# Nine modulation blocks among the pool chunks instead of five, and every third tile of the first norm modulated by VectorE

## The reference

```python
for l in range(DEPTH):                                  # DEPTH = 2
    ada = jax.nn.silu(cond) @ w_ada[l] + b_ada[l]       # 1024 x 6144 weights a layer
    sh1, sc1, g1, sh2, sc2, g2 = jnp.split(ada[:, None, :], 6, axis=-1)
    u = layer_norm(x) * (1 + sc1) + sh1
    if l % 2 == 0:
        m, k, v = even_mixer(u, ...)                    # attention beside a pool mixer
    else:
        m = odd_mixer(u, ...)                           # gated conv beside a Fourier mixer
    x = layer_norm(DEEPNORM_ALPHA * x + g1 * (m @ w_out[l]), ln_g[l, 0], ln_b[l, 0])
    u = layer_norm(x) * (1 + sc2) + sh2
    f = conv_ffn(u, w_up[l], ffn_conv_w[l], ffn_conv_b[l], w_down[l])
    x = layer_norm(DEEPNORM_ALPHA * x + g2 * f, ln_g[l, 1], ln_b[l, 1])
```

## Time and profile before

| what | value |
|---|---|
| median of three runs | 2673.08 us (2669.34 to 2676.3) |
| the profiled execution | 2669.81 us |
| its span | 2668.0 us |
| TensorE busy | 2564.1 us, 96% of the span |
| VectorE busy | 1608.6 us, 60% |
| ScalarE busy | 1067.2 us, 40% |
| GpSimd busy | 462.8 us, 17% |
| moved by DMA | 294.43 MB, mean 110 GB/s |

### The profile page before, as it was taken

One profiled execution on the slowest core, in us unless ns is written; L12 is line 12 of the kernel. 1 busy time (PEld: TensorE's weight loads), 2 busy tenths in 40 slices (PEclk: granted clock), 3 DMA queues, 4 the chain that ended last, 5 costly groups with the idle time before them and its releaser, 6 DMA issues. The chain is left out here.

```text
span 2668.0 us, 35753 instructions
## 1 busy us (share of the span) xinstructions
PE 2564.1 (96%) x13380; PEld 2284.1 (86%) x13380; DVE 1608.6 (60%) x2415; ACT 1067.2 (40%) x1691; POOL 462.8 (17%) x269
## 2 busy tenths in 40 slices
PE   5799799999999999999999999999999999999998
PEld 2488588778999999987777999988999999997886
DVE  2326677768866666644676533257866666654665
ACT  4412577846433233333645511126533332323442
POOL 1160377726000000000222000016100000000212
PEclk7889799999999999999999999999999999999999
DMA  9920100023222222255665312122322222245564
GB/s 326 340 74 15 55 1 1 1 96 111 72 62 67 70 74 74 58 200 186 240 246 191 106 40 75 58 80 87 90 74 74 74 74 71 61 168 171 198 213 142
DMA packets 209365, 294.43 MB, mean 110 GB/s; under 512 B 11529, under 2 KB 146677, under 8 KB 209263
## 3 DMA queue, kind: packets, MB, share of 16 engines
q1 hardware_dynamic: 205892, 284.10, 32.5%
q0 software_dynamic: 2736, 8.01, 0.8%
q10 hardware_dynamic: 635, 0.94, 0.1%
HBM read 247.73 MB, written 45.29 MB: 110 GB/s over the span
## 5 line engine op out<-in xcount | busy, mean ns | idle before, releaser
L2988 PE MATMUL ps<-d_ring,hs 128*128 128x512 f32 x2376 | 557.8, 395 | 1.9 <-PE ps L2988 1.3
L2988 PEld LDWEIGHTS ps<-d_ring,hs 128*128 128x128 f32 x2376 | 445.8, 188 | 113.9 <-issue 9.4
L1741 DVE TENSOR_TENSOR d_ring<-d_raw,d_ring 128x1024 fp32r<-128x1024 f32 x132 | 180.7, 1369 | 227.3 <-ACT hs L1054 226.9
L1036 POOL TENSOR_TENSOR ey<-ey,gb_end 128x1024 f32<-128x1024 f32 x17 | 44.1, 2592 | 1490.0 <-ACT ey L1559 1490.0
L2831 PE MATMUL ps<-act_b,w_A 128*128 128x384 f32 x1584 | 282.4, 336 | 2.9 <-ACT fp L1054 1.6
L2831 PE MATMUL ps<-act_a,w_A 128*128 128x384 f32 x1584 | 282.4, 336 | 2.9 <-ACT fp L1054 1.6
L2831 PEld LDWEIGHTS ps<-act_a,w_A 128*128 128x128 f32 x1584 | 275.2, 188 | 3.6 <-ACT fp L1054 1.9
L2831 PEld LDWEIGHTS ps<-act_b,w_A 128*128 128x128 f32 x1584 | 275.1, 188 | 3.6 <-ACT fp L1054 1.9
L1054 ACT ACTIVATE d_ring<-d_raw 128x1024 fp32r<-128x1024 f32 x132 | 139.8, 1059 | 286.0 <-PE ps L2988 249.8
L2619 PE MATMUL ps<-act_b,uw 128*128 128x384 f32 x1440 | 250.8, 336 | 1.5 <-DVE act_b L1741 1.2
L2619 PEld LDWEIGHTS ps<-act_b,uw 128*128 128x128 f32 x1440 | 249.4, 188 | 2.2 <-DVE act_b L1741 1.5
(11 more groups left out here) (284 smaller groups left out, 4252.1 us busy)
## 6 DMA issues: line engine op xcount, KB each, us to landing
d_raw<-in_w_down SPq DMA_DIRECT2D x132, 512.0 KB, 3.4
ada_w<-in_w_ada SPq DMA_DIRECT2D x52, 512.0 KB, 6.6
h_rows<-fh SPq DMA_DIRECT2D x44, 576.0 KB, 3.6
h_raw<-h_rows SPq DMA_DIRECT2D x132, 192.0 KB, 3.7
raw_u<-in_w_up SPq DMA_DIRECT2D x44, 512.0 KB, 5.4
raw_odd<-in_w_up SPq DMA_DIRECT2D x40, 512.0 KB, 4.9
end_w<-in_w_ada SPq DMA_DIRECT2D x24, 512.0 KB, 7.5
late_w<-in_w_ada SPq DMA_DIRECT2D x20, 512.0 KB, 6.9
```

Of the source, the lines that this page charges most:

```text
L1036: chain(gp.tensor_tensor(y, y, gb_end[l][:, 0, :], ALU.mult))
L1741: return v.tensor_tensor(dst, src, hi.bitcast(F32), ALU.subtract)
L2988: mm = pe.matmul(out, h[:, a, tile % 3 * P:(tile % 3 + 1) * P], d[:, w, 512 * half:512 * half + 512], start=f == 0 and (a, w) == (0, 0), s ...
```

## The change

- Five modulation blocks (4 to 8) stay in the first norm and nine (9 to 17) go among the pool chunks: `ADA_LATE` is 9. `FIRST_ADA` puts the five behind the turns of tiles 0, 2, 3, 5 and 6; `LATE_CHUNKS` then has one late block behind each chunk from (0, 1) to (3, 0). Banks, evacuation steps and SP's order follow: SP's loop over the norm's rows is written out, with no block behind every third tile, and its late loads stand among the weight loads.
- Tiles 2, 5 and 8 are modulated by VectorE out of the same PSUM banks into a second row `in_u2`; ScalarE still rounds them.
- All four column products of the second norm and of layer 1 come behind the last pool chunk, from four buffers `bias_row`; the rotary tables wait for them.
- In the FFN's `behind`, `third(0, 1)` and `first_product(0, 1)` stand ahead of the roundings of S3 and S1.

```diff
-    return {s: [s + 2] for s in range(2, 11)} if kind == "in" else {}
+    return {2: [4], 4: [5], 5: [6]} if kind == "in" else {}
-ADA_LATE = 13
+ADA_LATE = 9
+def ada_bank_of(m):
+    if m < ADA_TOP:
+        return 3 + m % 3
+    return 5 if m == ADA_TOP else 3 + (m - ADA_TOP - 1) % 2
+FIRST_ADA = {0: 4, 2: 5, 3: 6, 5: 7, 6: 8}
+        in_u2 = at("in_u2", [P, D], F32, off_s + 32768)
-        bias_row = [at(f"bias_row{i}", [P, D], F32, off_s + 20480 + 4096 * i) for i in range(2)]
+        bias_row = [at(f"bias_row{i}", [P, D], F32, off_s + 20480 + 4096 * i) for i in range(4)]
...
+                if i1 is None:
+                    for tile in range(NT - 3):
+                        step(tile, tile % 3, tile // 3 + 1)
+                        if tile % 3 < 2:
+                            ada_units(5 + tile // 3 * 2 + tile % 3)
+                    return
...
-            late_units(13)
-            bias_rows(range(2, 4), ADA_LATE)
+            late_units(9)
+            u_unit(2, u_source(2))
+            late_units(10)
+            wq_unit(0)
+            wq_unit(1)
+            late_units(11)
+            u_unit(3, u_source(3))
             wq_unit(2)
             wq_unit(3)
-            for m in (14, 15, 16):
-                late_units(m)
+            late_units(12)
+            late_units(13)
             wq_unit(4)
             wq_unit(5)
-            late_units(17)
-            bias_rows(range(4, 6), ADA_LATE + 1)
+            late_units(14)
+            late_units(15)
             wq_unit(6)
             wq_unit(7)
+            late_units(16)
+            late_units(17)
             wkv_unit(0)
             wkv_unit(1)
+            bias_rows(range(2, 6), 14)
             wkv_unit(2)
             wkv_unit(3)
...
+            sp.wait_ge(brow_mm, 6)
             for i in range(2):
                 sp.dma_start(rope_t[:, i, :, :], ...)
...
-                if s.live(2):
+                if s.live(2) and s.slot(2) < 2:
...
-                        act.wait_ge(act_rdy, tile)
+                        act.wait_ge(act_rdy, tile if s.slot(2) else tile - 1)
...
+                    self.third(0, 1)
+                    self.first_product(0, 1)
                     act.wait_ge(t_lo, t_until(l, 2))
                     self.hi(0, 1, "S3")
                     self.hi(0, 1, "S1")
-                    self.third(0, 1)
-                    self.first_product(0, 1)
...
+                    if s.slot(2) == 2:
+                        v.wait_ge(zt_done, tile + 1)
+                        v.wait_ge(act_rdy, tile - 2)
+                        for k in range(KD):
+                            o = v.tensor_scalar(in_u2[:, k * P:(k + 1) * P], ps[:, 6 + k // 4, (k % 4) * P:(k % 4 + 1) * P],
+                                                cols[:, 0, 1, k, 0:1], cols[:, 0, 0, k, 0:1], ALU.mult, ALU.add)
+                        o.then_inc(mod_done, 1)
...
-                if n == 1:
-                    cols_of(range(2, 4))
...
-            cols_of(range(4, 6))
+            cols_of(range(2, 6))
...
-                    ada_block(ADA_TOP + tile)
+                    if tile in FIRST_ADA:
+                        ada_block(FIRST_ADA[tile])
...
-                if n in (1, 3):
+                if n == U_FOUR - 1:
                     pe.wait_ge(ada_bank, 3 + ADA_END)
-                    cols_mm(range(n + 1, n + 3))
+                    cols_mm(range(2, 6))
```

More of the change, by code:

```diff
@@ L370, in build @@
         ada_st = [sem(f"ada_st{i}") for i in range(3)]
-        brow = [sem(f"brow{i}") for i in range(2)]
+        brow = [sem(f"brow{i}") for i in range(4)]
         brow_mm, cols_done = sem("brow_mm"), sem("cols_done")
@@ L590, in d_unit, with ada_units @@
                 sp.dma_start(raw_d[:, n % 2, 0:width], src).then_inc(d_loaded[n % 2], 16)
-            def ada_units(m, i=None):
+            def ada_units(m):
                 l, half = ada_half(m)
-                col = half * 512 if i is None else i * 1536 + half * 512
                 w = t["w_ada"][l].rearrange("(u kk p) n -> u p kk n", kk=2, p=P)
@@ L598, in ada_units @@
                     a = 4 * m + u
-                    sp.wait_ge(ada_used, a + 1 if i is None else i * 12 + (a + 1))
-                    sp.dma_start(ada_w[:, a % ADA_SLOTS, :, :], w[u][:, :, bass.ds(col, 512)]).then_inc(ada_ld[a % ADA_SLOTS], 16)
+                    sp.wait_ge(ada_used, a + 1)
+                    sp.dma_start(ada_w[:, a % ADA_SLOTS, :, :], w[u][:, :, half * 512:half * 512 + 512]).then_inc(ada_ld[a % ADA_SLOTS], 16)
             def late_units(m):
@@ L1078, in top_evac @@
                 act.wait_ge(ada_used, ADA_SLOTS + 4 * m + 4)
-                copy(ada_top[:, m, :], ps[:, 3 + m % 3, :]).then_inc(ada_bank, 1)
+                copy(ada_top[:, m, :], ps[:, ada_bank_of(m), :]).then_inc(ada_bank, 1)
             def late_evac(m):
@@ L1196, in first_norm @@
                     act.wait_ge(mod_done, tile + 1)
-                    copy(act_a[:, :, 0, bass.ds(tile * P, P)], in_u[:].rearrange("p (k t) -> p k t", k=KD)).then_inc(act_hi, 1)
+                    u = in_u2 if s.slot(2) == 2 else in_u
+                    copy(act_a[:, :, 0, bass.ds(tile * P, P)], u[:].rearrange("p (k t) -> p k t", k=KD)).then_inc(act_hi, 1)
                 if s.live(0):
@@ L1783, in ada_evac @@
                 used = ADA_SLOTS + 4 * m + 4
-                v.wait_ge(ada_used, used if i is None else i * 12 + used)
+                v.wait_ge(ada_used, used if i is None else i * 8 + used)
                 if i is not None:
-                    row = ada_row[:, bass.ds(i * 3 + (m - 5), 1), :].rearrange("p a n -> p (a n)")
+                    row = ada_row[:, bass.ds(i * 2 + (m - 5), 1), :].rearrange("p a n -> p (a n)")
                 else:
                     row = ada_side[:, (4, 11, 12).index(m), :]
-                v.tensor_copy(row, ps[:, 3 + m % 3, :]).then_inc(ada_bank, 1)
+                v.tensor_copy(row, ps[:, ada_bank_of(m), :]).then_inc(ada_bank, 1)
             def halves(x):
@@ L1887, in first_norm @@
                     tile = s.tile(2)
+                    if s.slot(2) == 2:
[5 more added lines that the diff above has]
+                        o.then_inc(mod_done, 1)
                     v.wait_ge(act_hi, tile + 1)
-                    lo(act_a[:, :, 1, bass.ds(tile * P, P)], in_u[:].rearrange("p (k t) -> p k t", k=KD), act_a[:, :, 0, bass.ds(tile * P, P)]).then_inc(act_rdy, 1)
+                    u = in_u2 if s.slot(2) == 2 else in_u
+                    lo(act_a[:, :, 1, bass.ds(tile * P, P)], u[:].rearrange("p (k t) -> p k t", k=KD), act_a[:, :, 0, bass.ds(tile * P, P)]).then_inc(act_rdy, 1)
                 if s.i is None and s.base < 2:
@@ L2477, in ada_block @@
             def ada_block(m):
-                pe.wait_ge(ada_bank, m + 1)
+                pe.wait_ge(ada_bank, m + 1 if m < ADA_TOP else m + 2)
                 for u in range(0, 4, 2):
@@ L2483, in ada_block @@
                         a, kk = 4 * m + u + q // 2, q % 2
-                        mm = pe.matmul(ps[32 * q:32 * q + 32, 3 + m % 3, :], conds[:, 2 * (2 * u + q):2 * (2 * u + q) + 32], ada_w[:, a % ADA_SLOTS, kk, :],
+                        mm = pe.matmul(ps[32 * q:32 * q + 32, ada_bank_of(m), :], conds[:, 2 * (2 * u + q):2 * (2 * u + q) + 32], ada_w[:, a % ADA_SLOTS, kk, :],
                                        start=u == 0, stop=u == 2)
@@ L2511, in cols_mm @@
                 for n in ns:
-                    pe.wait_ge(brow[n % 2], 32 * (n // 2))
+                    s = (n - 2) % 4
+                    pe.wait_ge(brow[s], 64 if n >= 6 else 32)
                     pe.wait_ge(cols_done, n - 1)
                     for k in range(KD):
-                        mm = pe.matmul(ps[:, 6 + n % 2, 2 * k:2 * k + 2], bias_row[n % 2][0:ADA_ROWS + 1, k * P:(k + 1) * P], con[0:ADA_ROWS + 1, C_SELC:C_SELC + 2],
+                        mm = pe.matmul(ps[:, 6 + n % 2, 2 * k:2 * k + 2], bias_row[s][0:ADA_ROWS + 1, k * P:(k + 1) * P], con[0:ADA_ROWS + 1, C_SELC:C_SELC + 2],
                                        start=True, stop=True)
```

18 lines of the change are left out of this document (6 added, 12 removed).

## The result

The changed kernel takes 2654.95 us, the median of four runs (2654.17 to 2658.08), against 2672.37 (2669.34 to 2676.3) for the kernel before beside it: a ratio of 0.994, with a 95% interval of 0.9929 to 0.9952. It is faster by 0.6%. The prediction said 2660, range 2651 to 2671, and that it would be faster. The profiled execution took 2658.08 us with a span of 2655.9, where before it was 2669.81 and 2668.0: 12.1 us less in the span. That execution is the slowest of its four, and the one of before (2669.81) lies 2.6 us under its median, so the medians lie further apart (17.4 us) than the two traces; a trace can account for its own 12.1 only.

A forecast was written before the change was run, and what follows sets the result against it. The front part was taken as two serial parts, about 142 us paced by loads, then 38 us of TensorE work with empty queues. Gains of 11.4 + 1.8 = 13.2 us gave 2660 us, range 2651 to 2671.

The forecast's parts named there:

- T9: Start of the first late modulation block, after the first norm's turns and two pool chunks: 94 us, ends 91 and 98.
- VectorE's tile: First norm: tiles modulated by VectorE, eight modulations at 2.65 us against 2.90 on ScalarE; no gain in itself.
- What it spares is the wait for the shared row: First norm: VectorE's modulation avoids waiting until the shared row is copied and split, 5.68 us between ScalarE modulations.
- The period: Pool stage: time from one late block to the next, 7.0 us, eight times; ends 6.64 and 7.65.
- The end of 6.64 for TensorE's own work: Pool stage: lower end of the period, a chunk of 4.44 us plus a late block of 2.20.
- loads no limit: Rival, pool stage: TensorE's 6.64 us sets the period, gain 14.3 + 1.8, time 2657 us; chance 0.15.
- loads alone: Rival, front part: loads alone set the end and never pause, gain 20.4 + 1.8, time 2651 us; chance 0.1.
- starved: Rival, pool stage: late buffers refill too slowly, at 9.3 us every period the time is 2678 us; chance 0.1.
- The tail: Front part from the last late block's start: block, two chunks, four column products, 19.7 us; ends 18.6 and 23.3.
- a gain at 181.13 as one at the end: First projection, at 181.13 us before: time gained there, 11.4 us, was taken to remain at the kernel's end.
- The FFN: Second FFN block: ScalarE's earlier first product shortens TensorE's wait, 0.9 us per layer, 1.8 in all; ends 0 and 3.2.
- shifted alike: Expected sign in the profile after: everything from the first projection on moves by the same amount.

The follow-up runs named there:

- e3: Changed kernel with ScalarE modulating all nine tiles of the first norm into the one buffer; 2652.19 us, ratio 0.9927 to the kernel before.
- e4: Kernel before with only VectorE's modulation of every third first-norm tile into the second buffer added; 2676.24 us, ratio 1.0017 to the kernel before.
- e8: Changed kernel with late blocks' loads beyond the first six cut to half their columns, not a usable kernel; 2651.62 us in one run.
- e9: Changed kernel with four buffers for the late blocks' weights in place of six; 2669.16 us, ratio 0.9988 to the kernel before.
- e2: Changed kernel with the FFN's reordering undone, so the front part alone; 2661.89 us, ratio 0.9965 to the kernel before.
- e1: Kernel before with ScalarE's new order in the FFN alone, both layers; 2666.01 us, ratio 0.9983 to the kernel before.
- e6: Changed kernel with ScalarE modulating every tile, every third into the second buffer; 2650.27 us, ratio 0.9923 to the kernel before.
- e10: Changed kernel with VectorE's modulation moved to the head of its step, ahead of the statistics; 2652.62 us, ratio 0.993 to the kernel before.
- e7: Changed kernel with ScalarE modulating every tile, every third into the second buffer, and column products split behind two late pool chunks; 2652.57 us, ratio 0.9935 to the kernel before.

## Why the prediction was right or wrong

**T9, predicted 94, measured 95.97.** The times of the chain came out step by step: turn 2 predicted at 51.5 (50.91), turn 3 at 59.8 (59.73), turn 6 at 79 (78.56), turn 8 at 88.4 (89.23). But what held VectorE ahead of turns 3 and 6 was not what the prediction had. It let VectorE wait for the rows of tiles 4 and 7, to 53.4 and 72.7 us; in the trace VectorE waits for neither, and starts the statistics at 53.62 and 72.79 right behind the low part of an earlier tile, which ends at 53.71 and 72.87 and has waited for ScalarE's rounding. That the two agree is luck. The term that was mis-sized is the chunk behind turn 8: it was priced at the 4.44 us of a chunk at full clock, and took 5.78, since the clock was down behind the idle 4.51 us ahead of that turn (0.67 granted from 90 to 95 us). With the 0.8 of turn 8 that makes about the 2.0.

**VectorE's tile.** "What it spares is the wait for the shared row" is the step that failed. The times of turns 3 and 6 came out right, but they were read as the best that the norm could do. e3 shows that without VectorE, with one row, turn 3 comes at 56.69 us, and e4 that VectorE's tile alone costs the kernel before 4.2 us. The prediction had even written down the order that does it, statistics, scale and eviction ahead of the modulation, and took it for a given; it should have priced ScalarE's way beside it. The cost per edit was hidden in a T9 that summed two edits with opposite signs.

**The period, predicted 7.0, measured 6.93.** Near, and the loads do lengthen it (e8, e9), but the agreement is in part luck. The eight periods are not alike: four take 6.23 to 6.55 us with no wait shown, four 7.07 to 7.79. The 7.0 was read in the trace of before between second halves; from start to start the same blocks (127.03 and 139.77) are 6.4 apart. The same front part in e2 has 6.69. The end of 6.64 for TensorE's own work was too high by 0.41. The rivals "loads no limit" and "loads alone" are out, as TensorE waits for late weights in some periods and not in others; "starved" at its price of 9.3 us in every period is out with six buffers.

**The tail, predicted 19.7, measured 21.27.** The chunks and the last block came as priced (10.4 against 11.1). The column products were priced at 8.6, from one pair at the full clock and one in between, and took 10.96: with all four together the clock falls in the middle of them. The prediction saw that risk, and kept it for the end of its range (23.3).

**First projection: predicted 169.7, measured 172.66; and "a gain at 181.13 as one at the end".** Of the 8.4 us at the first projection 7.1 are left where layer 0's output projection ends: the projection starts at the lower clock (0.50 from 170 to 175 us), and the attention's falls of the clock lie elsewhere. In e2, the same front part, they are 10.8 and 9.9. So by the traces the front part, predicted at 11.4, was over-rated by some 1.5 to 4.3 us, by the cold chunk, the column products and the slow start of the projection; the runs of e2 alone (6.1 to 12.6) would not tell it.

**The FFN, predicted 1.8, measured 5.0 in the trace (4.9 by e1's median).** The waits themselves came as worked out: 1.63 to 0.80 in both layers, 0.73 predicted, so 1.7 us. What the prediction had no term for is the clock. With one wait in layer 0 shortened, the clock stayed up behind the next wait, 1.6 us, and 2.7 more came at the output projection of layer 1, less 1.6 by the fall that then comes behind the wait for `ln_z`. That makes 4.4 of the 5.0; the rest has no row of its own. The sentence that everything behind the projection would be "shifted alike" failed, and the prediction's own test shows it: the shift grows at two places that the change doesn't touch and shrinks at a third.

**The total** of 13.2 against 12.1 in the traces is therefore partly luck: 4.3 too much in front and 3.2 too little behind. What stays firmly right is the shape: the front part ran as two serial parts, the move overlapped them, and nothing new became the limit. How much of it is the blocks' move by itself no run tells, as the column products' new place goes with it in all of them. That the medians differ by 17.4 where the traces differ by 12.1 is the spread of the runs.

Of the kernels here, e6 (2650.27), e10, e3 and e7 beat both the kernel before and the changed one by their medians; e6 and e3 need less code than the changed kernel, and the intervals of the four overlap with each other's and with the changed kernel's.

## What to carry to other kernels

When an engine is given a job of another engine, look at what stands ahead of the job in the new engine's order, and price the plain alternative too: here the instructions were as fast (2.63 against 2.90 us) and the place put the next turn 4 us later. Price each edit of a change by itself, as two that share one landmark can hide a loss in a gain. A stall of 1.63 us in a TensorE-bound stretch was worth more than itself here, as the granted clock fell behind the next stall; and a fall that is gone at one stall can come back at a later one. So read the clock in the stretches behind a stall before it is priced, and again in the new trace.

## What the runs showed of the hardware that was not expected

- The granted clock fell to 1.2 GHz in the midst of TensorE's column products, with no idle time between them: 64 products of two columns took 10.96 us, 32 of them at full clock 3.73, and in 165 to 170 us the clock was 0.50 with TensorE busy all of the 5.00 us.
- Shortening a wait from 1.63 to 0.80 us changed the clock behind another wait, of 2.07 us, 34 us later: 2.35 us for twelve products in ten kernels with the short wait in layer 0, 3.10 to 3.37 in the four with the long one.
- The clock fell behind exactly one of two waits of TensorE 90 us apart (1.50 and 2.06 us) in each of fourteen kernels: 96 products of 24.58 to 24.84 us and then 48 of 11.17, or 22.05 to 22.10 and then 12.58 to 12.79.
- The same front part in two kernels (after and e2) reached the first projection 2.4 us apart (172.66 and 170.34), by the waits for late weights and by where the clock fell in the column products. A difference of that size between two traces need not be the change's.
